# An attention kernel with values ahead of the next transposes, even filler, key-value latents first and four V buffers

## Chip, core and metric

One core of a Trainium2 chip. Its engines run side by side and meet at semaphores: TensorE (PE, matrix products and transposes into PSUM), VectorE (DVE), ScalarE (ACT), GpSimd (POOL, which doesn't reach PSUM), and SyncE (SP), which issues DMAs; ACT issues some too. The metric is the time of one execution on the device in microseconds.

## The reference

Two layers of a decoder trunk, for a prompt of 1024 tokens and 8 sample tokens that share all weights. What matters here is the attention branch of the prompt:

```python
def mla_qk(c_q, c_kv, k_r, pos, q_norm_g, w_uq, kv_norm_g):
    q = (rms_norm(c_q, q_norm_g) @ w_uq).reshape(B, T, N_HEADS, QK_HEAD)
    q_rope = rope(q[..., QK_NOPE:], pos)
    lat = rms_norm(c_kv, kv_norm_g)
    k_rope = rope(k_r[:, :, None, :], pos)[:, :, 0, :]
    ...
def mla_prompt(q_nope, q_rope, lat, k_rope, w_uk, w_uv):
    k_nope = jnp.einsum('bsc,chd->bshd', lat, w_uk)
    v = jnp.einsum('bsc,chd->bshd', lat, w_uv)
    def one_block(args):
        s = (q_nope . k_nope + q_rope . k_rope) * SM_SCALE
        s = jnp.where(k_pos[None, :] <= q_pos[:, None], s, -jnp.inf)
        p = jax.nn.softmax(s, axis=-1)
        return jnp.einsum('bhqk,bkhd->bqhd', p, v)
```

`c_q` (384 wide), `c_kv` (256) and `k_r` (32) are products of the layer's input with columns of `w_in`; the result is gated by a sigmoid-gated product (`ag`). The sample tokens attend to a paged cache; a pooling branch, the output products and layer norms follow.

## The kernel before

**Precision.** Every operand is held as a high and a low part (`XH`, `XL`; `CNH`, `CNL`; `KH`, `KL`; `QH`, `QL`; `PTH`, `PTL`), and a product is three products. ACT writes a high part, DVE subtracts for the low one.

**Weights** stream through a ring of four slots. SP loads a piece (`slab`), POOL splits it into high and low (`split`, L437), PE uses it in `unit` (L514) or `fill` (L533) and frees the slot (`w_used`). The order of `SLABS` is the order on all three engines.

**Latents and gates** (L685 to L704). Six units of 72 products make three query latents, two key-value latents and the rotary key; four more make the gates. Units alternate between two sets of three PSUM banks; a unit waits until the set is free (`unit_free`). ACT copies each latent to `CR` and its square to `SQ`; DVE adds squares; `squares` on PE sums over partitions; ACT takes roots; DVE takes the reciprocal and scales (L1165 to L1171), ACT and DVE make the parts; for each gate ACT takes a sigmoid, DVE multiplies and frees the banks.

**Values stage** (L706 to L726, L911 to L936). For each of 8 token blocks PE transposes latents and makes V; ACT copies the high part to `VSTG` (two buffers), copies `OUTT`, and issues three DMAs, one of them the spill of `VSTG` to HBM.

**The attention loop**, once for each of 4 head pairs in each of 2 layers (a pass). A pass has 16 blocks n: two heads of 8 blocks of 128 queries; block j of a head has (j+1)x128 keys. What each engine does, in the order written out by hand:

- PE (L741 to L757): `scores` 0 and 1, 24 filler products, then for each n `turn(n)` (transposes of the normalised block), `scores(n+2)`, at even n from 2 `values(n/2-1)`, and filler by `FILL_AT`. The filler is a product of the later mixing stage (144 products a pass), in six chunks that share one PSUM bank; ACT evacuates a chunk to `FST` and issues its DMA (`fill_evac`). After the loop: `keys_unit` of the next pair, `values(7)`, two query units.
- ACT (L972 to L993), iteration n: copies block n-2's transposes (`PTH`), takes the exponential of block n (`PB`), at even n from 4 copies `OB`, and at some n evacuates filler.
- DVE (L1230 to L1254), iteration n: reciprocal `RC` of n-1; mask, row maximum `MX` and `NB` of block n; `PTL` of block n-2 in one or two parts; at even n from 4 `ON`.
- POOL (L470 to L490): the normalising multiply of each block by `RC`, weight splits between.

`turn(n)` waits for POOL's multiply n and for `PTL` of n-1, whose PSUM banks it overwrites; `PTH` at even n waits for `values(n/2-1)`, which reads the buffer.

## Time and profile before

| | |
|---|---|
| median of 3 runs | 2287.74 us (2281.82 to 2289.15) |
| the profiled execution, whole | 2287.42 us |
| its span | 2285.5 us |
| mean granted clock of PE | 0.966 |
| busy: PE / DVE / ACT / POOL | 2051.3 / 910.4 / 508.6 / 755.3 us |
| chain that ended last: PE / DVE / issue / ACT | 78% / 11% / 5% / 2% |

The span runs from the first to the last instruction; the rest of the execution lies around it. Busy shares are averages over stages of different kinds, so the prediction reads single stages. In a timeline a bracket behind a row is the engine's idle time ahead of it and what ended that.

### The profile page before, as it was taken

Reading aid. Unit: us, or ns where it says so; the run is one execution under the profiler, and the core shown is the slowest. Engines: PE = TensorE matmul, PEld = TensorE weight load, DVE = VectorE, ACT = ScalarE, POOL = GpSimd, SP = SyncE. Lnnn points to the kernel's source line nnn. Section 1 sums busy time; section 2 is a strip of 40 time slices with the busy share of each in tenths; the row PEclk is TensorE's granted clock in tenths of the full one; section 3 lists DMA queues with packets and bytes.
Section 4 is the critical chain, followed back from the end, with each engine's and each line's share of the span. In section 5 each row is a group of like instructions: output and inputs, shape, how many; then the busy total and the mean of one; then the engine's idle time right before and its main releaser. Section 6 shows DMA issues by size and latency. Waiting matters only on the chain.

```text
span 2285.5 us, 33778 instructions
## 1 busy us (share of the span) xinstructions
PE 2051.3 (90%) x12406; PEld 1856.9 (81%) x12406; DVE 910.4 (40%) x1488; ACT 508.6 (22%) x895; POOL 755.3 (33%) x761
## 2 busy tenths in 40 slices
PE   2998898889998999999869988898799999999995
PEld 2997788774398999999869878788626989999994
DVE  7064555552155111421251645555423541133216
ACT  3122444441010100200121234444311110120002
POOL 5332333230034333443253233234200433334434
PEclk9999999998999999999979999999899999999997
DMA  3214011117312221111111231012461122211121
GB/s 113 61 42 148 26 55 60 54 55 235 135 44 64 79 74 55 42 46 51 47 31 45 68 117 57 26 55 66 155 213 54 49 86 65 74 42 47 50 62 76
DMA packets 90956, 167.08 MB, mean 73 GB/s; under 512 B 11641, under 2 KB 36489, under 8 KB 90415
## 3 DMA queue, kind: packets, MB, share of 16 engines
q1 hardware_dynamic: 74244, 135.43, 19.3%
q10 hardware_dynamic: 16572, 29.89, 3.5%
q8 instruction: 76, 1.25, 0.2%
q14 instruction: 64, 0.52, 0.1%
HBM read 141.74 MB, written 24.00 MB: 73 GB/s over the span
## 4 chain that ended last, share of the span: by engine, by line
PE 78%; DVE 11%; issue 5%; ACT 2%; DMA 2%; SPq 1%; ACTq 1%; DVEq 0%; POOL 0%; POOLq 0%
PE PS L525 53%; PE PS L546 6%; PE PS L568 4%; PE PS L616 3%; PE PS L646 2%; PE PS L579 2%; PE PS L603 2%; DVE MX L1239 2%; DVE PTL L1246 2%; PE PS L619 1%; PE PS L671 1%; DVE RT L1167 1%; DMA LATN<-out_lat_s 1%; PE PS L585 1%; DVE PS L1238 1%
## 5 line engine op out<-in xcount | busy, mean ns | idle before, releaser
L444 POOL CAST WH<-RAW 128x512 fp32r<-128x512 f32 (+3 forms) x296 | 192.4, 650 | 1079.4 <-DMA RAW<-in_wstream 1079.4
L446 POOL TENSOR_TENSOR WL<-RAW,WH 128x512 fp32r<-128x512 f32 (+3 forms) x296 | 381.9, 1290 | 23.9
L525 PE MATMUL PS<-XH,WH 128*128 128x344 f32 x1632 | 352.3, 324 | 13.9 <-DVEq L1349 5.5
L525 PE MATMUL PS<-XH,WL 128*128 128x344 f32 x1632 | 349.0, 322 | 0.0
L525 PE MATMUL PS<-XL,WH 128*128 128x344 f32 x1632 | 348.9, 322 | 0.0
L525 PEld LDWEIGHTS PS<-XH,WH 128*128 128x128 f32 x1632 | 275.9, 190 | 18.1 <-DVEq L1349 7.2
L525 PEld LDWEIGHTS PS<-XH,WL 128*128 128x128 f32 x1632 | 276.9, 190 | 0.0
L525 PEld LDWEIGHTS PS<-XL,WH 128*128 128x128 f32 x1632 | 276.3, 190 | 0.0
L467 POOL TENSOR_SCALAR PB<-PB,RC 128x128 f32<-128x128 f32 (+7 forms) x128 | 95.6, 747 | 346.6 <-DVE RC L1233 346.6
L579 PE MATMUL PS<-IDENT,PB 128*128 128x128 f32 x416 | 70.5, 284 | 77.6 <-DVE PTL L1246 77.6
L579 PEld LDWEIGHTS PS<-IDENT,PB 128*128 128x128 f32 x416 | 47.5, 143 | 96.8 <-issue 94.9
L546 PE MATMUL PS<-XH,WH 128*128 128x344 f32 x384 | 126.0, 328 | 0.0
L546 PE MATMUL PS<-XH,WL 128*128 128x344 f32 x384 | 122.7, 320 | 0.0
L546 PE MATMUL PS<-XL,WH 128*128 128x344 f32 x384 | 122.6, 319 | 0.0
L988 ACT ACTIVATE PB<-PS,NB 128x128 f32<-128x128 f32 (+7 forms) x128 | 94.9, 742 | 120.8 <-DVE NB L1240 119.8
L855 ACT ACTIVATE PTH<-PS 128x512 fp32r<-128x512 f32 (+1 forms) x192 | 87.3, 489 | 144.2 <-PE PS L603 116.7
L1373 DVE TENSOR_TENSOR SGP<-PS,SGP 128x1032 f32<-128x1032 f32 x16 | 19.7, 1233 | 246.4 <-PE PS L525 246.4
L1239 DVE TENSOR_REDUCE MX<-PS 128x1 f32<-128x128 f32 (+7 forms) x128 | 97.0, 757 | 4.4
L454 POOL TENSOR_TENSOR HT<-HT,GB 128x1024 f32<-128x1024 f32 (+1 forms) x27 | 70.1, 2611 | 75.1 <-ACT HT L868 63.1
L1246 DVE TENSOR_TENSOR PTL<-PS,PTH 128x512 fp32r<-128x512 f32 (+3 forms) x128 | 74.7, 584 | 48.5 <-ACT PTH L855 48.5
L603 PE MATMUL PS<-PTH,VSP 128*128 128x256 f32 x320 | 83.5, 292 | 3.1 <-DVE PTL L1250 3.1
L568 PE MATMUL PS<-KH,QH 128*128 128x512 f32 (+1 forms) x192 | 75.2, 392 | 8.4 <-DVEq L1212 8.2
(212 smaller groups left out, 3561.2 us busy)
## 6 DMA issues: line engine op xcount, KB each, us to landing
RAW<-in_wstream SPq DMA_DIRECT2D x232, 256.0 KB, 2.7
PGR<-in_pages SPq DMA_DIRECT2D x96, 320.0 KB, 4.9
PGA<-in_pages SPq DMA_DIRECT2D x32, 320.0 KB, 4.6
spill_g<-FST ACTq DMA_DIRECT2D x48, 172.0 KB, 1.9
SGL<-spill_g ACTq DMA_DIRECT2D x16, 516.0 KB, 4.4
spill_v<-VSTG ACTq DMA_DIRECT2D x16, 512.0 KB, 2.8
VSP<-spill_v SPq DMA_DIRECT2D x8, 1024.0 KB, 5.8
out_y_all<-HT SPq DMA_DIRECT2D x8, 512.0 KB
```

The source lines that it names most:

```text
L444: pool.tensor_copy(WH[:, slot, 0:size], RAW[:, slot, 0:size]).then_inc(w_high[slot], 1)
L446: pool.tensor_tensor(WL[:, slot, 0:size], RAW[:, slot, 0:size], f(WH[:, slot, 0:size]), ALU.subtract).then_inc(w_split[slot], 1)
L467: pool.tensor_scalar(PB[:, n % 2, 0:keys], PB[:, n % 2, 0:keys], RC[:, n:n + 1], 1.0, ALU.mult, ALU.mult).then_inc(nm_done, 1)
L525: last = nc.tensor.matmul(PS[:, 3 * par + c, 0:CH], w[:, slot, at], x(k)[:, c * CH:(c + 1) * CH], start=(k == 0 and n == 0), stop=(k == kt ...
L546: last = nc.tensor.matmul(PS[:, FILL_BANK, 0:CH], w[:, slot, (k % 4) * P:(k % 4 + 1) * P], x[:, k, c * CH:(c + 1) * CH], start=(step == 0) ...
L568: last = nc.tensor.matmul(score_banks(n)[:, c:c + w], q[:, h, j * P:(j + 1) * P], k[:, h, c:c + w], start=(m == 0), stop=(m == 2))
L579: last = nc.tensor.transpose(PS[:, 6, kb * P:(kb + 1) * P], PB[:, n % 2, kb * P:(kb + 1) * P], IDENT[:])
L603: last = nc.tensor.matmul(PS[:, o_bank(g), lo:2 * P], VSP[:, kb, h * P:(h + 1) * P], pt[:, kb, lo:2 * P], start=(kb == 0 and m == 0), stop ...
L855: return nc.scalar.activation(dst, src, ACT.Copy)
L988: nc.scalar.activation(PB[:, n % 2, 0:keys], score_banks(n)[:, 0:keys], ACT.Exp, bias=NB[:, n:n + 1], scale=SCALE, accum_out=SUM[:, n:n + ...
L1239: own(v.tensor_reduce(MX[:, n:n + 1], row[:, 0:(j + 1) * P], AX_X, ALU.max))
L1246: v.tensor_tensor(PTL[:, 0:w, c0:c0 + P], PS[:, 6, 0:w * P].rearrange("p (k c) -> p k c", c=P), f(PTH[:, 0:w, c0:c0 + P]), ALU.subtract).t ...
```

## The change

**Latents.** The two key-value latents are the first two units, the rotary key the third, the query latents the last three. `squares`, roots, sums, scalings and parts follow in the new order: three key-value squares after units 3 and 4, three query squares after gates 0 and 1. DVE scales the key-value latents ahead of gate 0 and the query latents between gates 1 and 2. The values stage waits for the key-value parts alone; the query units wait for the rest.

**V.** `VSTG` and its semaphores become four.

**Loop.** On PE `values(n/2-1)` stands ahead of `turn(n)`. The filler is 8 products for each n from 0 to 14, and its evacuations stand at n = 1, 4, 7, 10, 13, 16. On DVE `PTL` of block n-2 is first in iteration n. On POOL the next keys' weights are split at n = 9, both query slabs after the loop. SP gets some extra semaphore increments.

```diff
@@ -53,7 +53,7 @@
-SLABS = ([("c", 0, KD, 4, 1)] + [("c", n, KD, 2, 1) for n in range(1, 6)]
+SLABS = ([("c", KQ, KD, 4, 1)] + [("c", n, KD, 2, 1) for n in (*range(KQ + 1, KQ + KC + 1), *range(KQ))]
@@ -71,6 +71,8 @@
+ROPE_UNIT = KC
+LATENTS = ((0, KQ), (1, KQ + 1), (3, 0), (4, 1), (5, 2))
@@ -168,7 +170,7 @@
-        VSTG = at("VSTG", 19 * ROW, [P, 2, PAIRS, 4, V_DIM], F32R)
+        VSTG = at("VSTG", 19 * ROW, [P, 4, PAIRS, 4, V_DIM], F32R)
@@ -236,7 +238,8 @@
-        vs_out, fill_out, gate_in = ([sem(n + "0"), sem(n + "1")] for n in ("vs_out", "fill_out", "gate_in"))
+        vs_out = [sem(f"vs_out{k}") for k in range(4)]
+        fill_out, gate_in = ([sem(n + "0"), sem(n + "1")] for n in ("fill_out", "gate_in"))
@@ -290,9 +293,8 @@
-        FILL_AT = {-1: (0, 24), 0: (24, 36), 1: (36, 48), 2: (48, 60), 3: (60, 72), 4: (72, 78), 5: (78, 84),
-                   6: (84, 90), 7: (90, 96), 8: (96, 108), 9: (108, 120), 10: (120, 132), 11: (132, 144)}
-        FILL_EVAC = {1: 0, 3: 1, 5: 2, 9: 3, 11: 4, 13: 5}
+        FILL_AT = {-1: (0, 24)} | {n: (24 + 8 * n, 32 + 8 * n) for n in range(15)}
+        FILL_EVAC = {1: 0, 4: 1, 7: 2, 10: 3, 13: 4, 16: 5}
@@ -358,10 +362,12 @@
-                    for b in range(2):
-                        sp.wait_ge(vs_out[b], 64 * l + 64 + 1)
+                    for b in range(4):
+                        sp.wait_ge(vs_out[b], 32 * l + 32 + 1)
+                    sp.sem_inc(spare, 1)
...
+                    sp.sem_inc(spare, 1)
@@ -479,15 +485,11 @@
-                        if n == 5:
+                        if n == 9:
...
-                        if n == 13:
-                            split(l, after + 1, only=0)
-                        if n == 15:
-                            if i < PAIRS - 1:
-                                split(l, after + 2)
-                            else:
-                                split(l, after + 1, only=1)
+                    split(l, after + 1)
+                    if i < PAIRS - 1:
+                        split(l, after + 2)
@@ -675,29 +677,33 @@
 
                 def squares(n):
 
-                    par, c = divmod(n, 3)
-                    pe.wait_ge(sq_sum, 2 * l + par + 1)
+                    part, c = divmod(n, 3)
+                    pe.wait_ge(sq_sum, 2 * l + part + 1)
                     if n >= 2:
                         pe.wait_ge(rt_ready, 6 * l + n - 1)
-                    nc.tensor.matmul(PS[:, 6 + n % 2, 0:CH], ONES[:], SQ[:, (KQ - 1, KQ + KC - 1)[par], c * CH:(c + 1) * CH],
+                    nc.tensor.matmul(PS[:, 6 + n % 2, 0:CH], ONES[:], SQ[:, (KQ + KC - 1, KQ - 1)[part], c * CH:(c + 1) * CH],
                                      start=True, stop=True).then_inc(ss_done, 1)
 
                 for s in range(B_G):
                     unit(l, s, rows(XH), rows(XL))
-                    if s >= 4:
-                        squares(2 * (s - 4))
-                        squares(2 * (s - 4) + 1)
+                    if s == 3:
+                        squares(0)
+                        squares(1)
+                    if s == 4:
+                        squares(2)
 
                 for m in range(PAIRS):
                     unit(l, B_G + m, rows(XH), rows(XL))
                     if m == 0:
+                        squares(3)
                         squares(4)
+                    if m == 1:
                         squares(5)
 
                 pe.wait_ge(kr_ready, l + 1)
-                pe.wait_ge(cn_ready, (KQ + KC) * (l + 1))
-                pe.wait_ge(ch_ready, (KQ + KC) * (l + 1))
-                pe.wait_ge(cl_ready, (KQ + KC) * (l + 1))
+                pe.wait_ge(cn_ready, (KQ + KC) * l + KC)
+                pe.wait_ge(ch_ready, (KQ + KC) * l + KC)
+                pe.wait_ge(cl_ready, (KQ + KC) * l + KC)
                 pe.wait_ge(unit_free[0], q_of(l, B_G + 2) + 2)
                 slots = [piece_of(l, B_V, k) for k in range(KC)]
                 for slot, q in slots:
@@ -735,6 +741,8 @@
                     unit(l, B_F + 5 * i + 2, rows(CNH), rows(CNL))
 
                 keys_unit(0)
+                pe.wait_ge(ch_ready, (KQ + KC) * (l + 1))
+                pe.wait_ge(cl_ready, (KQ + KC) * (l + 1))
                 query_units(0)
                 for i in range(PAIRS):
                     r = l * PAIRS + i
@@ -742,11 +750,11 @@
                     scores(l, i, 1)
                     fill(l, i, -1)
                     for n in range(16):
+                        if n >= 2 and n % 2 == 0:
+                            values(r, n // 2 - 1)
                         turn(r, n)
                         if n + 2 < 16:
                             scores(l, i, n + 2)
-                        if n >= 2 and n % 2 == 0:
-                            values(r, n // 2 - 1)
                         fill(l, i, n)
                     pe.wait_ge(fill_free, 6 * r + 6)
                     if i < PAIRS - 1:
@@ -878,43 +887,63 @@
-                for s in range(KQ + KC):
+                def latent(s, k):
...
-                    copy(thirds(CR[:, s, :]), bank_set(s % 2))
-                    nc.scalar.activation(thirds(SQ[:, s, :]), bank_set(s % 2), ACT.Square).then_inc(unit_free[s % 2], 1)
+                    copy(thirds(CR[:, k, :]), bank_set(s % 2))
+                    nc.scalar.activation(thirds(SQ[:, k, :]), bank_set(s % 2), ACT.Square).then_inc(unit_free[s % 2], 1)
...
+                def root(n):
...
+                    part, c = divmod(n, 3)
+                    act.wait_ge(ss_done, 6 * l + n + 1)
+                    nc.scalar.activation(RT[:, 1 - part, c * CH:(c + 1) * CH], PS[:, 6 + n % 2, 0:CH], ACT.Sqrt, bias=EPSC[:],
+                                         scale=1.0 / (KV_LORA, Q_LORA)[part]).then_inc(rt_ready, 1)
...
+                def high(n):
...
+                    k = LATENTS[n][1]
+                    act.wait_ge(cn_ready, (KQ + KC) * l + n + 1)
+                    copy(CNH[:, k, :], CR[:, k, :]).then_inc(ch_ready, 1)
...
-                for n in range(6):
-                    par, c = divmod(n, 3)
-                    act.wait_ge(ss_done, 6 * l + n + 1)
-                    nc.scalar.activation(RT[:, par, c * CH:(c + 1) * CH], PS[:, 6 + n % 2, 0:CH], ACT.Sqrt, bias=EPSC[:],
-                                         scale=1.0 / (Q_LORA, KV_LORA)[par]).then_inc(rt_ready, 1)
...
-                for k in range(KQ + KC):
-                    act.wait_ge(cn_ready, (KQ + KC) * l + k + 1)
-                    copy(CNH[:, k, :], CR[:, k, :]).then_inc(ch_ready, 1)
-                    if k in (KQ - 1, KQ + KC - 1):
-                        gate(k // KQ)
+                latent(*LATENTS[0])
+                latent(*LATENTS[1])
+                latent(*LATENTS[2])
+                root(0)
+                root(1)
+                latent(*LATENTS[3])
+                root(2)
+                latent(*LATENTS[4])
+                high(0)
+                high(1)
+                gate(0)
+                root(3)
+                root(4)
+                root(5)
+                gate(1)
+                for n in range(KC, KQ + KC):
+                    high(n)
...
-                    act.dma_start(SPILL_V[t * P:(t + 1) * P, :], f(VSTG[:, t % 2]).rearrange("p i s d -> p (i s d)")
-                                  ).then_inc(vs_out[t % 2], 16)
+                    act.dma_start(SPILL_V[t * P:(t + 1) * P, :], f(VSTG[:, t % 4]).rearrange("p i s d -> p (i s d)")
+                                  ).then_inc(vs_out[t % 4], 16)
...
-                        act.wait_ge(vs_out[par], 64 * l + 16 * (t // 2) + 1)
-                        copy(values_high(VSTG[:, par]), PS[:, t % 3, :].rearrange("p (i x d) -> p i x d", i=PAIRS, x=2)
+                        act.wait_ge(vs_out[t % 4], 32 * l + 16 * (t // 4) + 1)
+                        copy(values_high(VSTG[:, t % 4]), PS[:, t % 3, :].rearrange("p (i x d) -> p i x d", i=PAIRS, x=2)
@@ -1130,21 +1159,20 @@
-                for par, k in ((0, 1), (0, 2), (1, 4)):
...
-                    dve.wait_ge(unit_free[k % 2], q_of(l, k) + 2)
-                    dve.wait_ge(unit_free[1 - k % 2], q_of(l, k - 1) + 2)
-                    last = v.tensor_tensor(SQ[:, k, :], SQ[:, k, :], SQ[:, k - 1, :], ALU.add)
-                    if k == 1:
-                        own(last)
-                    else:
-                        last.then_inc(sq_sum, 1)
+                def sum_squares(n):
...
+                    (s, k), (before, other) = LATENTS[n], LATENTS[n - 1]
+                    dve.wait_ge(unit_free[s % 2], q_of(l, s) + 2)
+                    dve.wait_ge(unit_free[before % 2], q_of(l, before) + 2)
+                    return v.tensor_tensor(SQ[:, k, :], SQ[:, k, :], SQ[:, other, :], ALU.add)
...
+                sum_squares(1).then_inc(sq_sum, 1)
...
-                products(dve, l, 5)
-                v.tensor_tensor(thirds(T1[64:96, :]), bank_set(1, 96, P), thirds(TAB[96:P, :]), ALU.mult)
-                own(v.tensor_tensor(thirds(T2[64:96, :]), bank_set(1, 64, 96), thirds(TAB[64:96, :]), ALU.mult))
-                dve.sem_inc(unit_free[1], 1)
+                products(dve, l, ROPE_UNIT)
+                v.tensor_tensor(thirds(T1[64:96, :]), bank_set(0, 96, P), thirds(TAB[96:P, :]), ALU.mult)
+                own(v.tensor_tensor(thirds(T2[64:96, :]), bank_set(0, 64, 96), thirds(TAB[64:96, :]), ALU.mult))
+                dve.sem_inc(unit_free[0], 1)
@@ -1162,28 +1190,42 @@
-                for par, lo, hi in ((0, 0, KQ), (1, KQ, KQ + KC)):
-                    dve.wait_ge(rt_ready, 6 * l + 3 * par + 3)
-                    own(v.reciprocal(RT[:, par, :], RT[:, par, :]))
-                    for k in range(lo, hi):
-                        v.scalar_tensor_tensor(out=CR[:, k, :], in0=CR[:, k, :], scalar=GL[:, k:k + 1], in1=RT[:, par, :],
+                def scaled(part):
...
+                    lo, hi = ((0, KC), (KC, KQ + KC))[part]
+                    dve.wait_ge(rt_ready, 6 * l + 3 * part + 3)
+                    own(v.reciprocal(RT[:, 1 - part, :], RT[:, 1 - part, :]))
+                    for _, k in LATENTS[lo:hi]:
+                        v.scalar_tensor_tensor(out=CR[:, k, :], in0=CR[:, k, :], scalar=GL[:, k:k + 1], in1=RT[:, 1 - part, :],
...
-                    gate(par)
...
+                def low(n):
...
+                    k = LATENTS[n][1]
+                    dve.wait_ge(ch_ready, (KQ + KC) * l + n + 1)
+                    v.tensor_tensor(CNL[:, k, :], CR[:, k, :], f(CNH[:, k, :]), ALU.subtract).then_inc(cl_ready, 1)
...
+                own(sum_squares(3))
+                scaled(0)
+                sum_squares(4).then_inc(sq_sum, 1)
+                low(0)
+                low(1)
+                gate(0)
+                gate(1)
+                scaled(1)
+                gate(2)
+                for n in range(KC, KQ + KC):
+                    low(n)
+                gate(3)
...
-                for k in range(KQ + KC):
-                    dve.wait_ge(ch_ready, (KQ + KC) * l + k + 1)
-                    v.tensor_tensor(CNL[:, k, :], CR[:, k, :], f(CNH[:, k, :]), ALU.subtract).then_inc(cl_ready, 1)
-                gate(2)
-                gate(3)
-                dve.wait_ge(cn_ready, (KQ + KC) * (l + 1))
...
-                        last = v.tensor_tensor(VSTG[:, t % 2, :, 1 + x, :],
+                        last = v.tensor_tensor(VSTG[:, t % 4, :, 1 + x, :],
...
-                                               f(VSTG[:, t % 2, :, 3 * x, :]), ALU.subtract)
+                                               f(VSTG[:, t % 4, :, 3 * x, :]), ALU.subtract)
@@ -1228,16 +1270,6 @@
 
                     own = Chain(dve, own_v["mx"], 32, r)
                     for n in range(18):
-                        if 1 <= n <= 16:
-                            dve.wait_ge(ex_done, 16 * r + n)
-                            v.reciprocal(RC[:, n - 1:n], SUM[:, n - 1:n]).then_inc(rc_done, 1)
-                        if n < 16:
-                            h, j = BLOCKS[n]
-                            row = score_banks(n)
-                            dve.wait_ge(sc_done, 16 * r + n + 1)
-                            own(v.tensor_tensor(row[:, j * P:(j + 1) * P], row[:, j * P:(j + 1) * P], MASK[:], ALU.add))
-                            own(v.tensor_reduce(MX[:, n:n + 1], row[:, 0:(j + 1) * P], AX_X, ALU.max))
-                            v.tensor_scalar(NB[:, n:n + 1], MX[:, n:n + 1], -SCALE, None, ALU.mult).then_inc(mx_done, 1)
                         m = n - 2
                         if m >= 0:
                             j = BLOCKS[m][1]
@@ -1250,6 +1282,16 @@
+                        if 1 <= n <= 16:
+                            dve.wait_ge(ex_done, 16 * r + n)
+                            v.reciprocal(RC[:, n - 1:n], SUM[:, n - 1:n]).then_inc(rc_done, 1)
+                        if n < 16:
+                            h, j = BLOCKS[n]
+                            row = score_banks(n)
+                            dve.wait_ge(sc_done, 16 * r + n + 1)
+                            own(v.tensor_tensor(row[:, j * P:(j + 1) * P], row[:, j * P:(j + 1) * P], MASK[:], ALU.add))
+                            own(v.tensor_reduce(MX[:, n:n + 1], row[:, 0:(j + 1) * P], AX_X, ALU.max))
+                            v.tensor_scalar(NB[:, n:n + 1], MX[:, n:n + 1], -SCALE, None, ALU.mult).then_inc(mx_done, 1)
```

## Rows read from the trace of the kernel before

**Rows 1.** PE's waits over the run: line, releaser, us in total, times, longest.
```profile
PE PS L579 <- DVE PTL L1246: 77.6, 72, 2.5
...
PE PS L525 <- DVE OT L1161: 5.0, 3, 2.1
```

**Rows 2.** Busy time by engine from `turn` 0 to `turn` 15, pair 2.
```profile
382.12:439.73 57.61, 47.91 (x317) 43.65 (x314) 32.00 (x84) 26.78 (x63) 20.29 (x27) 1.00 0.09 28
```

**Rows 3.** PE timeline, end of pair 2: start us, us, operation, idle before.
```profile
435.91 0.63 PE L579 MATMUL PS<-IDENT,PB 128*128 128x128 f32 x4 [2.53 <-DVE PTL L1246]
...
439.73 0.63 PE L579 MATMUL PS<-IDENT,PB 128*128 128x128 f32 x4 [1.50 <-DVE PTL L1246]
...
443.47 0.28 PE L603 MATMUL PS<-PTH,VSP 128*128 128x256 f32 x1
...
445.29 0.68 PE L525 MATMUL PS<-CNH,WH 128*128 128x344 f32 x3
```

**Rows 4.** DVE timeline, end of pair 2.
```profile
433.76 1.22 DVE L1239 TENSOR_REDUCE MX<-PS 128x1 f32<-128x1024 f32 x1
435.01 0.15 DVE L1240 TENSOR_SCALAR NB<-MX 128x1 f32<-128x1 f32 x1
435.08 0.68 DVE L1246 TENSOR_TENSOR PTL<-PS,PTH 128x512 fp32r<-128x512 f32 x1
435.68 0.41 DVE L1250 TENSOR_TENSOR PTL<-PS,PTH 128x256 fp32r<-128x256 f32 x1
436.44 0.16 DVE L1233 RECIPROCAL RC<-SUM 128x1 f32<-128x1 f32 x1 [0.34 <-ACT PB L988]
...
441.02 0.69 DVE L1246 TENSOR_TENSOR PTL<-PS,PTH 128x512 fp32r<-128x512 f32 x1 [0.51 <-ACT PTH L855]
```

**Rows 5.** ACT timeline, start and end of pair 2.
```profile
382.41 0.46 ACT L855 ACTIVATE FST<-PS 128x344 f32<-128x344 f32 x1 [1.11 <-PE PS L546]
382.90 0.34 ACTq L958 DMA_DIRECT2D spill_g<-FST  x1
383.29 0.28 ACT L855 ACTIVATE PTH<-PS 128x128 fp32r<-128x128 f32 x1 [0.42 <-ACT FST L855]
...
430.44 1.01 ACT L988 ACTIVATE PB<-PS,NB 128x896 f32<-128x896 f32 x1
...
431.56 0.38 ACT L855 ACTIVATE OB<-PS 64x256 f32<-64x256 f32 x1
431.96 0.87 ACT L855 ACTIVATE PTH<-PS 128x512 fp32r<-128x512 f32 x2
435.20 1.11 ACT L988 ACTIVATE PB<-PS,NB 128x1024 f32<-128x1024 f32 x1 [2.37 <-DVE NB L1240]
...
440.39 1.09 ACT L855 ACTIVATE PTH<-PS 128x512 fp32r<-128x512 f32 x2 [0.75 <-PE PS L579]
```

**Rows 6.** DVE's maximum of 128 keys in pair 2, form by form: busy us, mean ns.
```profile
L1239 DVE TENSOR_REDUCE MX<-PS 128x1 f32<-128x128 f32 x1 | 0.3, 291 | 0.0
```

**Rows 7.** POOL timeline: the normalising multiply of block 15, pair 2.
```profile
436.80 1.13 POOL L467 TENSOR_SCALAR PB<-PB,RC 128x1024 f32<-128x1024 f32 x1 [3.00 <-DVE RC L1233]
```

**Rows 8.** The page's costliest groups: a weight piece's low part, mean ns.
```profile
L446 POOL TENSOR_TENSOR WL<-RAW,WH 128x512 fp32r<-128x512 f32 (+3 forms) x296 | 381.9, 1290 | 23.9
```

**Rows 9.** Chain that ended last, in order of time: a unit of 72 products.
```profile
118.58 11.39 PE PS L525 x72
```

**Rows 10.** PE timeline at the gates of layer 0.
```profile
157.13 0.74 PE L525 MATMUL PS<-XH,WH 128*128 128x344 f32 x3 [2.11 <-DVE OT L1161]
```

**Rows 11.** ACT timeline at the gates of layer 0.
```profile
153.48 1.28 ACT L889 ACT_TABLE_LOAD   x1
```

**Rows 12.** A window of layer 1 behind an idle time (PEclk: granted clock).
```profile
1278.30:1281.70 3.40, 3.40 (x14) 3.40 (x13) 3.40 (x1) 0.00 (x0) 1.89 (x2) 0.50 0.00 0
```

**Rows 13.** ACT timeline in the values stage of layer 0.
```profile
192.19 0.60 ACT L855 ACTIVATE VSTG<-PS 128x512 fp32r<-128x512 f32 x1 [2.75 <-DMA spill_v<-VSTG]
...
194.78 0.60 ACT L855 ACTIVATE VSTG<-PS 128x512 fp32r<-128x512 f32 x1 [1.68 <-issue]
```

13 lines of the change are left out of this document (8 added, 5 removed).

## Prediction

> **What bounds the kernel now.** I read the head of the page first (span 2285.5 us, TensorE (PE) busy for most of it, so only its idle time can be won), then PE's own waits over the whole run. The longest group by far is `turn` (L579) waiting for the low-part subtraction PTL on VectorE (DVE, L1246), 77.6 us in 72 waits, so 9.7 us in each of the 8 passes over a head pair; the gates' units wait 5.0 us for OT [rows 1]. Third, one pass at undisturbed clock (pair 2 of layer 0): from `turn` 0 to `turn` 15 it takes 57.61 us, in which PE is busy 47.91, DVE 32.00, ScalarE (ACT) 26.78 [rows 2]. No engine is full; the loop is held by a chain of hand-overs. Fourth, the timelines of one step. `turn` 14 starts at 435.91, 0.83 after the first PTL of block 13 began at 435.08 [rows 3, 4]. That PTL did not wait for its data: it stood behind mask, row maximum and NB of block 15 (maximum 433.76, NB 435.01), which waited for PE's scores. So today a step is: turn, scores, mask and maximum, PTL, next turn. The exponential runs beside PTL and costs that chain nothing.
>
> **The change in the attention loop.** DVE now takes PTL(m) ahead of RC(m+1) and of mask, maximum, NB of block m+2. PE no longer waits for a maximum before PTL. But the order on ACT is unchanged: the copy PTH(n-1) stands behind the exponential of block n, and that exponential needs NB(n), which now stands behind PTL(n-2). This closes a serial loop that before was open: PTL(n-2), RC, mask, maximum, NB on DVE; exponential n, whatever ACT does at the end of its iteration, PTH(n-1); PTL(n-1). I cost it from rows, from the end of one PTL to the end of the next:
> - hand-overs: RC 0.10 (0.16 long at 436.44, less its overlap with the next), mask 0.34 (my estimate: as a 128-wide maximum with its hand-over), maximum's tail 0.03, NB to exponential 0.19 (435.01 to 435.20): together 0.66 [rows 4, 5];
> - M, the maximum: 0.29 at 128 keys, 1.22 at 1024, on a line between [rows 4, 6];
> - E, the exponential: 1.01 at 896 keys and 1.11 at 1024, on the line through them down to 0.47 at 256, plus 0.12 where OB follows (430.44, OB at 431.56) [rows 5];
> - X, what follows it on ACT: OB 0.40 (431.56 to 431.96) at even n from 4; evacuating a filler chunk 0.88 (FST 382.41, its DMA issue 382.90, PTH 383.29) at n = 4, 7, 10, 13 by the new table [rows 5];
> - H, PTH to PTL: 0.63 at four or more blocks (440.39 to 441.02), down to 0.41 for two and 0.31 for one (my estimates, less by the 0.11 a block of the exponential) [rows 4, 5];
> - L, PTL: 0.60 for four blocks (435.08 to 435.68); with the second part 0.82 to 1.20; 0.22 for one (estimates: a part's duration runs with its width like the maximum's, less the 0.08 by which two overlap) [rows 4].
>
> ```
> n    M     E     X     H     L    0.66+sum
> 2   0.56  0.57   -    0.41  0.34   2.54
> 3   0.69  0.68   -    0.52  0.47   3.02
> 4   0.82  0.91  1.28  0.63  0.60   4.90
> 5   0.96  0.89   -    0.63  0.82   3.96
> 6   1.09  1.12  0.40  0.63  0.94   4.84
> 7   1.22  1.11  0.88  0.63  1.08   5.58
> 10  0.56  0.69  1.28  0.41  0.34   3.94
> 11  0.69  0.68   -    0.52  0.47   3.02
> 12  0.82  0.91  0.40  0.63  0.60   4.02
> 13  0.96  0.89  0.88  0.63  0.82   4.84
> 14  1.09  1.12  0.40  0.63  0.94   4.84
> 15  1.22  1.11   -    0.63  1.08   4.70
> ```
> Two steps go by another path. RC(k), too, now stands behind PTL(k-1), so the normalising multiply on GpSimd (POOL) comes in series: RC to its start 0.36 and 1.13 at 1024 keys [rows 4, 7], 0.15 to PE (a PTL of 0.68 lets `turn` start at 0.83 [rows 3, 4]). For k=7: 1.63, then turn to PTH 0.66 (439.73 to 440.39) [rows 3, 5], H, L 1.20: 4.12. For k=8 `values(3)` comes first: 1.82 long (443.47 to 445.29 for the same 16 products [rows 3]), with 0.15 ahead and `turn`, PTH and PTL of one block, 0.9, behind: in all 2.85. The 14 steps sum to 57.2. Ahead of them, `turn` 0 to PTL(0): 1.17 to PTH(0) (382.12 to 383.29 [rows 2, 5]), then about 0.5: 1.7. Behind them RC(15) and the multiply, 1.6, before `turn` 15. Total 60.5 against 57.61: **+2.9 a pass, +23.1 for eight**. `values` ahead of `turn` at even n is covered: it runs while the multiply makes the block that `turn` waits for. At every step but the eighth PE's work (8 fillers 1.26, scores up to 1.5, turn up to 0.8, values up to 1.8) is shorter than the loop beside it, so evening the fillers buys nothing.
>
> What is late next: after the loop `turn` 15, the keys unit, `values(7)` and two query units follow on PE alone, as today; they start 2.9 later.
>
> **Splits and loads.** POOL splits the next keys at n = 9 and both query slabs after n = 15. A piece of four tiles costs POOL 1.29 for its low part and about half of that for the high one [rows 8], so the two query pieces of three tiles take some 3 us after the last multiply, while PE has 0.8 of turn, 2.9 of keys unit (a quarter of a unit of 11.39 [rows 9]) and 1.8 of values ahead of the first query unit. Cost nothing; if the cover were gone, up to 3 a pass. SP's loads keep their order; the slots of the last two free one and two steps later than now, still before `turn` 15. The extra semaphore increments on SP cost nothing seen.
>
> **Latents first.** PE's own work is the same: six units, four gates and six squares a layer. Now the gate units wait 5.0 us (the longest 2.11 at 157.13) since DVE has a long queue of reciprocals and scalings between the gates [rows 1, 10]. In the new order DVE has little to do when gate 0's unit ends: table load 1.28, sigmoid and multiply about 1.1 each, done 3.5 us after it, 8 ahead of the end of the next unit (11.39), when its banks are wanted; gate 1's waits for a square and a root more, 4.7, so 6.7 ahead [rows 9, 11]. The 5.0 go. In layer 1 the 2.1 idle was followed by a stretch at half clock, 3.4 us, of which half is lost: 1.7 [rows 12]. Sum -6.7. Two more table loads on ACT each layer lie within those 6.7 us (1.28 each). The values stage then starts as soon as PE is there, as now.
>
> **Four V buffers.** ACT takes 2.6 a block by its own work; only one block a layer waits for a spill: idle 2.75 where its neighbour has 1.68, 1.07 more, and I take as much for layer 1 [rows 13]. The rest of the stage is ACT's issues, which stay. **-2.1** for two. Bounds: 0 (OUTT's own buffers wait instead) and 2.1.
>
> **Sum**, against the profiled run's own 2287.4 (span 2285.5; the median is 2287.7): 2287.4 + 23.1 - 6.7 - 2.1 = **2301.7**. Bounds of the loop's term: 0.1 us of error on each of 14 steps is 11 us over eight passes, so +12 to +34.
>
> **Rivals.**
> - *ACT's filler issue is free.* If the DMA issue and its gap (0.39 of the 0.88) don't hold the next copy, four steps a pass get shorter: -12.5, so **2289.2**, within the noise. Against it: PTH in the row comes only after the issue [rows 5]. The Trainium skill, "DMA: Bandwidth & Descriptors", section Issuing engines are not separate DMA queues, calls the sequencer's time to start a DMA usually small beside the DMA; by that rule this rival holds, while the row here shows 0.34 on the path.
> - *Faster: PTL first sets PE free.* The mechanism is what the 77.6 us suggest: PTL no longer waits behind a maximum, and the exponential is out of the way by the time the copy's data come. Then a step is the longer of PE's work (2.2 to 3.9) and the path of k=7 above, RC, multiply, turn, H, L (2.2 to 4.1): 47.5 for the 14 steps, 50.8 in all, -6.8 a pass, so 2287.4 - 54.4 - 8.8 = **2224**. It decides once the serial loop is under 54.3 for the 14 steps, 0.2 less in each. For it: neither DVE nor ACT is busy much over half the pass [rows 2]. Against it: both run their queues in order, and the code puts the exponential ahead of the copy.
> - *The clock.* PE will idle about 2.9 us ahead of `turn` 15, 2.5 ahead of `turn` 7. Today an idle time of 2.1 ahead of a gate unit in layer 1 is followed by 3.4 us at half clock [rows 12], and half of the passes lose their clock so once. If four passes more than today get it, 4 x 1.7, and all eight a second one at `turn` 7, partly covered, 8 x 1.2: up to +16.4, **2318**.
> - *The gates don't gain.* The new order only moves the idle time: +8.8, **2310.5**.
>
> **How the numbers follow.** Forecast 2302, chance 0.54; free issue 0.14; clock 0.16; no gain at the gates 0.06; faster 0.10. Range 2285 to 2318: it takes in the free issue, most of the clock case and the loop's bounds, and leaves out the fast case and the tails. About 0.3% (7 us) is what a measurement of this kernel can tell from no change. Slower by more: 0.75 (forecast, clock, gates, less a little); same: 0.14; faster: 0.11.
>
> **What would show it.** In the trace after: exponential n starting only after PTL(n-2), and PTH(n-1) right behind it, so that DVE and ACT alternate; `turn` 15 about 60.5 after `turn` 0; PE's waits at `turn` put down to the POOL multiply and not to PTL, and above 100 us in all; no wait at the gates; no ACT wait for spill_v. I'm wrong if PTH starts while the exponential of the next block is still to come, or if a pass is shorter than 57.6.

## The result and the profile after

The changed kernel takes 2332.85 us (median of 4 runs, 2327.55 to 2335.32); the kernel before, run beside it, 2286.2. The ratio is 1.0203 (95% interval 1.0177 to 1.0228): slower by 2.0%, 31 us more than the 2302 forecast and above the range. The profiled execution took 2331.88 (span 2330.0), 44.5 more than that of before.

PE's waits of the changed kernel over the whole run (line, releaser, us in total, times, longest):

```profile
PE PS L581 <- POOL PB L473: 63.3, 62, 2.4
PE PS L770 <- DMA LATN<-out_lat_s: 25.0, 2, 12.7
```

These answer to [rows 1]. `turn` (now L581) no longer waits for PTL but for the multiply, as foreseen; the total is smaller than the 77.6 of before, and yet the kernel is slower. The gates' wait for OT is gone. The second line is new: L770 is the first product of the sample stage with UKT, and it waits about 12.5 us in each layer for a DMA.

Passes, windows from `turn` 0 to `turn` 15 of pairs 2 and 3 of layer 0 (columns as in [rows 2]: length, then busy time and count of PE, PEld, DVE, ACT, POOL, granted clock, DMA share, GB/s):

```profile
384.84:447.06 62.22, 51.96 (x317) 46.16 (x314) 31.75 (x86) 26.85 (x63) 17.48 (x24) 0.95 0.07 24
466.95:526.90 59.95, 49.72 (x317) 43.51 (x314) 31.65 (x86) 26.84 (x63) 19.76 (x24) 1.00 0.10 34
```

A pass at full clock takes 59.9 to 60.0; the eight are 59.9, 62.4, 62.2, 60.0 and 61.0, 62.3, 59.9, 61.0, mean 61.07. In the kernel before a pass at full clock takes 57.6, as in [rows 2], and the mean of the eight is 58.49, since five of the eight lose 1.3 to 1.6 us of clock ahead of the last `turn`. The hand-overs at the end of pair 2, DVE and then ACT (start us, us, operation, idle before):

```profile
435.31 0.69 DVE L1278 TENSOR_TENSOR PTL<-PS,PTH 128x512 fp32r<-128x512 f32 x1 [2.50 <-ACT PTH L864]
...
436.49 1.09 DVE L1293 TENSOR_REDUCE MX<-PS 128x1 f32<-128x896 f32 x1
437.62 0.15 DVE L1294 TENSOR_SCALAR NB<-MX 128x1 f32<-128x1 f32 x1
...
439.96 0.69 DVE L1278 TENSOR_TENSOR PTL<-PS,PTH 128x512 fp32r<-128x512 f32 x1 [0.20 <-ACT PTH L864]
...
441.29 1.22 DVE L1293 TENSOR_REDUCE MX<-PS 128x1 f32<-128x1024 f32 x1
```

```profile
437.81 1.01 ACT L1017 ACTIVATE PB<-PS,NB 128x896 f32<-128x896 f32 x1 [2.37 <-DVE NB L1294]
...
438.93 0.38 ACT L864 ACTIVATE OB<-PS 64x256 f32<-64x256 f32 x1
439.33 0.87 ACT L864 ACTIVATE PTH<-PS 128x512 fp32r<-128x512 f32 x2
```

Against [rows 4, 5] PTL now comes first on DVE, and everything else waits in a row: PTL at 435.31, maximum 436.49, NB 437.62, exponential 437.81, OB 438.93, PTH 439.33, the next PTL 439.96. DVE and ACT alternate; the serial loop of the prediction is there, piece by piece.

SyncE's DMA issues at the end of the last pass of layer 0, first before, then after (start us, us from the first to the last issue of the group; SPq: its DMA queue):

```profile
472.72 31.67 SPq L333 DMA_DIRECT2D RAW<-in_wstream  x3
509.78 4.15 SPq L381 DMA_DIRECT2D PGA<-in_pages  x8
514.13 0.58 SPq L389 DMA_DIRECT2D UKT<-in_ukt  x1
514.81 0.52 SPq L390 DMA_DIRECT2D UVF<-in_uvf  x1
515.62 0.29 SPq L393 DMA_DIRECT2D LATN<-out_lat_s  x1
```

```profile
482.95 42.09 SPq L337 DMA_DIRECT2D RAW<-in_wstream  x4
530.39 4.68 SPq L387 DMA_DIRECT2D PGA<-in_pages  x8
535.26 0.57 SPq L395 DMA_DIRECT2D UKT<-in_ukt  x1
535.93 0.51 SPq L396 DMA_DIRECT2D UVF<-in_uvf  x1
536.73 0.29 SPq L399 DMA_DIRECT2D LATN<-out_lat_s  x1
```

And the chain that ended last, in order of time, over the same place in the kernel after:

```profile
523.28 1.28 PE PS L548 x8
524.71 0.33 SPq L337
525.05 0.05 issue
525.16 0.48 SPq L382
...
536.73 8.92 DMA LATN<-out_lat_s
545.65 0.04 issue
545.69 2.51 PE PS L770 x11
```

PE's last eight fillers (L548, n = 14) free a weight slot at 524.56; only then does SP issue the last piece of slab B_H + 1 (L337). Behind it in SP's program stand the reads of the page ids (L382), eight page loads, UKT, UVF and LATN, and LATN lands at 545.65. In the kernel before, the last filler was at n = 11, and LATN was issued at 515.62, 21.1 us earlier. From `turn` 15 (526.90) to the UKT products it is now 18.8 us, where it was 6.9; in layer 1, 19.6 and 6.8.

**Where the 44.5 us are** (profiled executions): from the first `turn` 0 to the last `turn` 15 of a layer +11.1 and +14.2; from there to the UKT products +11.9 and +12.8; everything ahead of the first `turn` 0 -3.0, from layer 0's UKT products to layer 1's first `turn` 0 -1.5; the rest -1.0.

### The profile page after: what moved, and what is told of

It is laid out like the page before. It is cut to its first block, busy times and chain, and to the rows that moved or that the text cites. A ratio compares the mean times of both kernels' runs of the same rounds, so it can differ in the third digit from the quotient of the medians.

```text
span 2330.0 us, 33806 instructions
## 1 busy us (share of the span) xinstructions
PE 2071.6 (89%) x12406; PEld 1866.3 (80%) x12406; DVE 908.5 (39%) x1488; ACT 513.9 (22%) x899; POOL 757.4 (33%) x761
## 4 chain that ended last, share of the span: by engine, by line
PE 68%; DVE 11%; issue 8%; ACT 7%; ACTq 2%; DMA 1%; SPq 1%; POOL 1%; DVEq 0%; POOLq 0%
PE PS L527 54%; DVE MX L1293 4%; PE PS L618 3%; PE PS L648 2%; ACT PTH L864 2%; ACT PB L1017 2%; PE PS L548 2%; PE PS L605 1%; PE PS L621 1%; DVE PS L1292 1%; PE PS L673 1%; DVE PTL L1282 1%; DMA LATN<-out_lat_s 1%; ACT FST L864 1%; POOL PB L473 1%
## 5 line engine op out<-in xcount | busy, mean ns | idle before, releaser
L527 PEld LDWEIGHTS PS<-XH,WH 128*128 128x128 f32 x1632 | 276.1, 190 | 12.8 <-DVEq L1391 7.2
L548 PE MATMUL PS<-XH,WH 128*128 128x344 f32 x384 | 127.8, 333 | 13.4 <-ACT FST L864 13.4
L581 PE MATMUL PS<-IDENT,PB 128*128 128x128 f32 x416 | 74.2, 293 | 63.3 <-POOL PB L473 63.3
L548 PE MATMUL PS<-XH,WL 128*128 128x344 f32 x384 | 125.0, 325 | 0.0
L548 PE MATMUL PS<-XL,WH 128*128 128x344 f32 x384 | 124.5, 324 | 0.0
L581 PEld LDWEIGHTS PS<-IDENT,PB 128*128 128x128 f32 x416 | 46.1, 144 | 80.3 <-POOL PB L473 80.1
L460 POOL TENSOR_TENSOR HT<-HT,GB 128x1024 f32<-128x1024 f32 (+1 forms) x27 | 70.2, 2615 | 75.1 <-ACT HT L877 63.3
L548 PEld LDWEIGHTS PS<-XH,WH 128*128 128x128 f32 x384 | 73.7, 192 | 23.5 <-ACT FST L864 22.2
```

The lines of the kernel that those rows point to most:

```text
L460: pool.tensor_tensor(HT[0:n, t, :], HT[0:n, t, :], GB[0:n, :], ALU.mult).then_inc(ht_mul, 1)
L527: last = nc.tensor.matmul(PS[:, 3 * par + c, 0:CH], w[:, slot, at], x(k)[:, c * CH:(c + 1) * CH], start=(k == 0 and n == 0), stop=(k == kt ...
L548: last = nc.tensor.matmul(PS[:, FILL_BANK, 0:CH], w[:, slot, (k % 4) * P:(k % 4 + 1) * P], x[:, k, c * CH:(c + 1) * CH], start=(step == 0) ...
L581: last = nc.tensor.transpose(PS[:, 6, kb * P:(kb + 1) * P], PB[:, n % 2, kb * P:(kb + 1) * P], IDENT[:])
```

## Experiments

"Pass" below is `turn` 0 to `turn` 15 in the trace of the run, "between" is from there to the next `turn` 0. Medians in us; ratios to the kernel before, run beside each.

### 1. SP's sample loads first

```diff
-                slab(l, B_H)
-                slab(l, B_H + 1)
 ...
                 sp.dma_start(LATN[...], ...)
+                slab(l, B_H)
+                slab(l, B_H + 1)
```

> The changed kernel with one move on SP: the first sample's pages, UKT, UVF and LATN are issued ahead of the first two pooling slabs instead of behind them. Theory Q (these loads stand in SP's queue behind a slab that waits for the last filler products, which now end at n = 14 instead of 11): PE's wait for LATN falls from 25.0 us to under 2, the whole falls by 22 to 26 us, to about 2309. Rival (the loads are late because the DMA engines are busy or because the page identifiers are slow to read): the wait stays within 3 us of 25. The passes stay at 61.1 in both.

Measured 2304.52, ratio 1.0076 (1.0059 to 1.0093), 28.3 less than the changed kernel, a little more than the 22 to 26 expected. LATN is issued at 473.90, PE no longer waits for it at all, and the UKT products start 6.3 us after `turn` 15 in both layers. The queue on SP is the cause of that part.

### 2. The old filler table under the new orders

```diff
-        FILL_AT = {-1: (0, 24)} | {n: (24 + 8 * n, 32 + 8 * n) for n in range(15)}
+        FILL_AT = {-1: (0, 24), 0: (24, 36), ... 11: (132, 144)}
```

> The changed kernel with the filler, its evacuations and POOL's splits as before; values first, PTL first, latents first and four buffers stay. Theory Q: the last filler product is at n = 11 again, the LATN wait of 25 us goes. Theory S (the pass is held by PTL, maximum, exponential, copy in series): the filler is not what lengthens the pass; evacuations stand at five n inside the chain instead of four, so a pass is 61 to 63. Whole: 2308 to 2320. Rival E (the even filler is what costs the loop): passes fall back to 58.5, whole about 2288.

Measured 2309.92 (1.0089 to 1.0123). SP's order is that of the changed kernel, yet the UKT products start 6.9 after `turn` 15: the late filler is what held SP. Passes are 60.3 to 61.3, so under the new orders the even filler buys nothing in the loop, as forecast. It does shorten PE's wait ahead of `turn` 15 from 3.6 to 4.0 us to 2.4 us.

### 3. PTL first alone

The kernel before, with only PTL(n-2) moved ahead of RC, mask, maximum and NB on DVE.

> The kernel before with one change: on DVE PTL(n-2) ahead of RC(n-1) and of mask, maximum and NB of n. Theory S: this alone closes the serial loop, and values behind scores now holds up the copy at even n too: a pass goes from 58.5 to about 64 (steps of 5.4 at n = 4, 12, 14 and 5.7 at n = 6), whole about 2286 + 47 = 2333. Rival (PTL first frees PE, and the loss comes from PE's new order): PE's wait at turn falls below 77.6 us and the whole is at or under 2286.

Measured 2363.79 (1.0319 to 1.0353): +77, where +47 was expected. Passes are 66.0 to 67.6. ACT's timeline in it:

```profile
517.38 0.19 ACT L988 ACTIVATION_READ_ACCUMULATOR PB<-PS,NB 128x1 f32 x1
518.31 0.98 ACT L855 ACTIVATE PTH<-PS 128x512 fp32r<-128x512 f32 x2 [0.74 <-PE PS L603]
```

The exponential ends at 517.57, and the copy then waits 0.74 for PE's `values` (L603): at even m PTH overwrites what `values` of the group before reads, and PE's old order puts `values` behind `turn` and scores. My expectation left that out. So values ahead is what the new DVE order needs: with this filler the two together give a mean pass of 60.8 (experiment 2), PTL first without values ahead 66.8.

### 4. Latents and V buffers alone

The changed kernel with orders, filler and splits of before.

> The changed kernel with the attention loop, filler and splits as before: only latents first and four V buffers are left of the change. By the traces: no wait at the gates (5.0 us before), passes 58.5 as before, no LATN wait; 2286 less 5 to 7, about 2280. Rival: the gain is taken back later in the layer (clock, values stage): within 2 us of before.

Measured 2280.48, ratio 0.9975 (0.9963 to 0.9986), -6.2. Experiments 4 and 1 cut the way from the kernel before to the changed one into three steps, in medians: 2286.7 - 6.2 (latents, V) + 24.0 (loop: 2304.5 - 2280.5) + 28.3 (SP) = 2332.8. The steps are differences of neighbouring runs, so they add up whatever the cause; the causes are shown by the traces. In this run's trace the stretches ahead of the first `turn` 0 of each layer (from the start, and from layer 0's UKT products) are 4.4 us shorter each, and its passes 0.34 longer in the mean (58.83), since only one keeps its clock where three did.

### 5. DVE's old order under values ahead

> The changed kernel with one thing put back: on VectorE, mask, maximum and NB of block n stand ahead of PTL(n-2) again, as in the kernel before. Values ahead of the next transposes, the even filler, the latents' order and the four V buffers stay. Theory S (the serial loop over DVE and ACT, closed by PTL first, is what lengthened the pass): passes from turn 0 to turn 15 fall from 61.1 to about 58, PE's largest wait at the turn is put down to PTL again, exponential n starts before PTL(n-2) ends; LATN still lands late (some 12 us ahead of each layer's sample stage), so the whole is about 2332.9 - 8 x 3.1 = 2308 (2300 to 2316). Theory P (PE's new order, values ahead of the turn, lengthened it): passes stay at 60 to 61, 2325 to 2333.

Measured 2327.65 (1.0149 to 1.0185); passes 60.3 and 60.4. Theory P, and a miss for the claim that DVE's order alone is to blame. DVE and then PE in it:

```profile
403.93 1.23 DVE L1281 TENSOR_REDUCE MX<-PS 128x1 f32<-128x1024 f32 x1
405.19 0.15 DVE L1282 TENSOR_SCALAR NB<-MX 128x1 f32<-128x1 f32 x1
405.26 0.68 DVE L1288 TENSOR_TENSOR PTL<-PS,PTH 128x512 fp32r<-128x512 f32 x1
405.85 0.41 DVE L1292 TENSOR_TENSOR PTL<-PS,PTH 128x256 fp32r<-128x256 f32 x1
```

```profile
406.32 0.39 PE L605 MATMUL PS<-PTH,VSP 128*128 128x256 f32 x1 [1.51 <-DVE PTL L1292]
...
407.78 0.41 PE L581 MATMUL PS<-IDENT,PB 128*128 128x128 f32 x2
```

`values` waits 1.51 us for PTL, which stands behind the next maximum, and `turn` starts 1.46 later, after `values`. At every even n the time of `values` now lies between PTL and `turn`; before it lay beside DVE's maximum. The steps agree: against experiment 6 those that end at an even n are longer, from 0.5 us (n = 2) to 2.4 (n = 8), and the steps from `turn` 6, 8 and 14 are shorter, by 1.3 to 1.6.

### 6. Even filler alone, SP mended

Latents first, four V buffers, even filler, SP's sample loads first; PE's and DVE's orders as before.

> Latents first, four V buffers and the even filler with its splits, but PE's and DVE's orders in the loop as in the kernel before, and SP's page, UKT, UVF and LATN loads ahead of the last two filler slabs. What is measured is the even filler alone, against the kernel before with latents first and four V buffers (2280.5). Theory: at turn 15 the kernel before waits 1.5 us on PTL(13) with no filler to cover it in steps 12 to 15; evened out, eight filler products a step take part of it: passes 57.1 instead of 58.8, 2280.5 - 8 x 1.7 = 2267 (2260 to 2275). Rival: with eight filler products in every step some steps become bound by PE or by the evacuation of a chunk, and nothing is won: 2278 to 2286. If the sample stage's operands are late still, +24.

Measured 2255.23, ratio 0.9849 (0.9827 to 0.987), faster than the kernel before by 33. In a window of pair 2 (columns as above):

```profile
371.85:427.97 56.12, 48.76 (x317) 43.29 (x314) 32.01 (x84) 26.69 (x63) 18.91 (x25) 1.00 0.07 23
```

All passes are 56.0 to 56.1, against a mean of 58.8 in experiment 4, whose one pass at full clock takes 57.6: 1.6 of the gain is waits that are filled (1.7 was expected), the other 1.2 the clock, which no pass loses any more. The eight passes make 22.4 of the 25.3 us against experiment 4; another 2.6 lie between `turn` 15 and the UKT products, where LATN comes early. So the even filler is good under PE's and DVE's old orders. Values ahead costs 4.3 a pass on top of it (60.3, experiment 5); PTL first on top of both takes 0.4 off a pass at full clock (59.9), but its longer waits cost clock, and the mean is 61.1.

### 7. Copy ahead of the exponential

To break the serial loop at ACT: PTH(n-1), then the exponential of block n.

```diff
-                        m = n - 2
-                        if m >= 0:
+                        for m in ((), (), (0, 1))[n] if n < 3 else (n - 1,) if n < 17 else ():
                             ... copy PTH of block m
                         if n < 16:
                             ... exponential of block n
```

> The changed kernel with ACT's loop turned round: copy PTH(n-1) stands ahead of the exponential of block n, where now the exponential comes first. No arithmetic changes. Theory S says the serial loop (PTL(n-2), mask, maximum, NB, exponential n, PTH(n-1), PTL(n-1)) is broken by it. What is left is PTH(n-1), exponential n, RC, multiply, turn, PTH(n): with the rows' durations 2.5 to 4.4 us a step, 50.6 for 14 steps, a pass of about 54 instead of 61; 2332.9 - 8 x 7 = 2276 (2265 to 2295), the late LATN unchanged. The rival, that the pass is held by the multiply and the turn and not by the queue order of ACT, says 60 to 62 a pass, 2325 to 2340. A third: the later exponential only puts the wait on RC, which stands ahead of the mask on DVE, and the pass comes out at 57 to 58, 2305.

> Both mends together: copy PTH(n-1) ahead of the exponential on ACT, and SP's page, UKT, UVF and LATN loads ahead of the last two filler slabs. They act at different places (inside the passes; between the last turn and the sample stage), so the times should add: 2304.5 (SP's order alone) - 8 x 7 = 2248, range 2240 to 2268. If the first does nothing, 2305.

Measured 2368.09 (1.0312 to 1.0363) and, with SP mended, 2341.2 (1.0213 to 1.0244); passes 62.0 to 63.6. Both far off. ACT and DVE in the first:

```profile
415.66 0.88 ACT L864 ACTIVATE PTH<-PS 128x512 fp32r<-128x512 f32 x2 [2.35 <-PE PS L581]
416.42 1.01 ACT L1016 ACTIVATE PB<-PS,NB 128x896 f32<-128x896 f32 x1
...
417.55 0.38 ACT L864 ACTIVATE OB<-PS 64x256 f32<-64x256 f32 x1
```

```profile
417.96 0.42 DVE L1267 TENSOR_TENSOR ON<-PS,OB 64x256 f32<-64x256 f32 x1 [2.90 <-ACT OB L864]
418.31 0.67 DVE L1277 TENSOR_TENSOR PTL<-PS,PTH 128x512 fp32r<-128x512 f32 x1
```

PTH is done at 416.54, but PTL starts at 418.31. DVE stood for 2.90 us at ON, which is ahead of PTL in its queue and waits for OB; OB stood behind the exponential. PE also waited 42.6 us for filler chunks, evacuated a turn later than before. The loop was not broken, only led over another operation.

### 8. OB and evacuation moved ahead too

```diff
+                        if n >= 4 and n % 2 == 0:
+                            own_low(r, n // 2 - 2)
+                        if n in FILL_EVAC:
+                            fill_evac(l, i, FILL_EVAC[n])
                         for m in ...   # copy PTH, then the exponential
```

> As the run with copy PTH(n-1) ahead of the exponential and SP's sample loads first (2341.2), but the copy OB and the evacuation of a filler chunk, which ACT did after the exponential, now stand ahead of PTH(n-1). Why that run missed, by my reading of its trace: ON on VectorE stands ahead of PTL(n-1) in its queue and waits for OB, which waited for the exponential, so the serial loop stayed closed at every even n; and PE waited 42.6 us for filler chunks evacuated a turn later than before. If so, both go here: step = PTH, exponential, RC, multiply, turn, 2.5 to 4.4 us, a pass of 54 to 56 instead of 62 to 63, whole 2304.5 - 8 x 6 = 2256 (2244 to 2270). Rival: the multiply and the turn in series hold every step whatever ACT does, pass 60 or more, 2300 to 2340.

Measured 2255.91 (0.9844 to 0.9877), as expected; undisturbed passes 54.2 against 59.9. Moving three operations in one engine's queue, with no work added or taken, changed the kernel by 49 us (2304.5 to 2255.9). That shows the serial loop as the cause of the long pass under the new orders. The run moves OB and the evacuation together, so it doesn't tell how much of experiment 7's loss each of them held.

### 9. Two V buffers, and experiment 6 again

> The kernel with the even filler, the old orders on PE and VectorE, latents first and SP's sample loads first (2255.2 in another call, run again beside this one), with two V buffers in place of four. Theory A, as forecast: the wait for a spill, 1.07 us a layer, comes back: +2.1 us. Theory B, from the trace after (where the wait for a spill is gone, but one DMA issue a layer took 1.5 to 1.9 us in place of 0.46): the stall only moves between wait and issue, so the difference is 0 +- 1. Both are near what three rounds tell; the trace decides: the values stage from its first to its last product in each layer.

> The even filler with the old orders on PE and VectorE, latents first, four V buffers and SP's sample loads first, again, beside the two above and in more rounds: 2255 +- 3, a ratio of 0.985 to 0.987 to the kernel before. If it comes out above 2265, the first measurement was a chip's luck.

Measured 2253.57 (2251.44 to 2257.36) with two and 2254.13 (2251.9 to 2256.82) with four: no difference, but four runs of each, spread over 5 to 6 us, can't tell 2.1 us from nothing. The changed kernel's ACT in the values stage, to answer to [rows 13], and then that of the run with two buffers:

```profile
184.28 1.88 ACTq L937 DMA_DIRECT2D spill_v<-VSTG  x1
186.32 0.60 ACT L864 ACTIVATE VSTG<-PS 128x512 fp32r<-128x512 f32 x1 [3.08 <-PE PS L726]
188.25 0.46 ACTq L937 DMA_DIRECT2D spill_v<-VSTG  x1
```

```profile
185.13 1.56 ACTq L938 DMA_DIRECT2D spill_v<-VSTG  x1
186.88 0.60 ACT L865 ACTIVATE VSTG<-PS 128x512 fp32r<-128x512 f32 x1 [2.78 <-PE PS L727]
```

The wait for a spill is gone, but an issue of the same DMA held ACT for 1.88 us where its neighbours take 0.46. The slow issue is not the price of four buffers, since it comes with two as well. The traces say more than the medians. From PE's first transpose of the stage to its last, the six stages of the three traces with two buffers (the kernel before, experiment 3 and this one) take 20.2 to 20.7 us. With four buffers the sixteen stages that have a slow issue take 20.1 to 21.8, and the six that have none 19.2 to 19.3 (layer 0 of the run with four buffers here among them). So 1.1 us a layer, the forecast 1.07, is won where no issue is slow, as far as six stages show; in most stages the slow issue takes it.

### 10. Filler where PE waits

Experiment 8 with 12 filler products after `turn` 6, 16 after `turn` 14, 4 in steps 0, 1 and 4. Four chunks, not two as the expectation has it, are evacuated a step later.

> The run with copy, OB and evacuation ahead of the exponential (2255.9), with filler products moved to where PE idles most: 12 in place of 8 after turn 6, 16 after turn 14, 4 in steps 0, 1 and 4, which have no idle time; the evacuation of two chunks a step later. PE's work is the same. In that run the undisturbed pass is 54.2, but in 5 of 8 passes idle time of 1.8 ahead of turn 7 is followed by about 1.3 us more in step 7, and idle time of 2.2 ahead of turn 15 by a keys unit of 4.6 in place of 3.1 us. Theory C (the half clock follows those idle times): they shrink to 1.2 and 0.9, the granted clock stays up, all passes 54 to 54.5, keys units 3.1: 8 us in the passes and 9 between them, 2239 (2232 to 2248). Rival: the half-clock stretches come at other idle times instead, or the extra products only lengthen steps 6 and 14: 2252 to 2262.

Measured 2243.52, ratio 0.9793 (0.9774 to 0.9813), the fastest of all. Windows of pair 2 and of the keys unit behind it, in experiment 8 and here (columns as above; the clock is the third number from the end):

```profile
373.28:429.17 55.89, 49.26 (x317) 44.98 (x314) 33.05 (x86) 26.54 (x65) 17.50 (x24) 0.97 0.08 25
429.17:433.20 4.03, 4.03 (x20) 4.03 (x21) 1.29 (x2) 1.08 (x2) 2.86 (x4) 0.64 0.16 60
```

```profile
369.11:423.38 54.27, 47.96 (x316) 43.45 (x314) 33.03 (x86) 26.39 (x65) 17.43 (x24) 1.00 0.07 24
423.38:427.40 4.02, 4.02 (x29) 4.02 (x30) 1.29 (x2) 1.13 (x3) 2.60 (x4) 1.00 0.41 107
```

With the waits of 1.8 and 2.2 us filled, the clock stays up: the pass is 1.6 shorter, the same 4 us do 29 products in place of 20, and "between", 21.4 to 21.5 in five cases of six, is 19.9 in all. The waits ahead of `turn` 7 and 15 are 1.21 and 0.92 (1.20 ahead of `turn` 15 in the first pass of each layer). The gain was 12 us of the 17 expected. My expectation had counted 5 of 8 passes of experiment 8 as losing clock at `turn` 7; its trace has that in two (steps of 5.94 and 5.92 us for 4.59). In the profiled executions the passes gain 5.4 us in all and the stretches between them 7.8.

The last pass of each layer keeps a long step, 4.40 and 4.41 us at n = 9 for 2.64 in the other passes. POOL and then PE in layer 0:

```profile
474.93 0.61 POOL L452 CAST WH<-RAW 128x512 fp32r<-128x512 f32 x1
...
477.55 1.27 POOL L454 TENSOR_TENSOR WL<-RAW,WH 128x512 fp32r<-128x512 f32 x1
478.80 0.58 POOL L475 TENSOR_SCALAR PB<-PB,RC 128x384 f32<-128x384 f32 x1
```

```profile
479.43 0.55 PE L583 MATMUL PS<-IDENT,PB 128*128 128x128 f32 x3 [1.59 <-POOL PB L475]
```

This is the split at n = 9. In the last pass the slab behind it is the first of the pooling branch, two pieces of four tiles, and it holds POOL for 3.9 us; for a keys slab, with pieces of one tile, it is 1.6. The multiply of block 10 stands behind it and `turn` 10 waits. Steps 9 and 10 together are 1.7 us longer than in the other passes, once a layer, now that the serial loop is open. In the changed kernel the loop hides nearly all of it: step 9 is 4.23 for 3.82 us, step 10 2.76 for 3.06.

## Why the prediction was wrong

**The step that failed** is in *Splits and loads*: "SP's loads keep their order; the slots of the last two free one and two steps later than now, still before `turn` 15. ... cost nothing". Both slots free three steps later, not one and two: the products that end them move from n = 10 and 11 to n = 13 and 14. They still free before `turn` 15 (the last at 524.56, `turn` 15 at 526.90). The conclusion, that this costs nothing, is what failed: I asked whether the weights would be in time, and not what else stands behind those two loads on SP. In the last pair that is the whole operand set of the sample stage, some 20 us of reads, issues and landing. The filler's end moved from n = 11 to 14, and the row moved with it. Price: 28.3 us in experiment 1, 24.6 in the profiled executions. The trace of before held the sign of it, among PE's waits (columns as in [rows 1]):

```profile
PE PS L762 <- DMA LATN<-out_lat_s: 1.4, 2, 0.8
```

PE already waited for LATN there, so there was no slack. The Trainium skill, "DMA: Bandwidth & Descriptors", section Issuing engines are not separate DMA queues, calls the sequencer's time to start a DMA usually small beside the DMA. For a single DMA the trace agrees: an issue of a page load takes 0.33 to 0.70 us, and the load lands 4.7 us after it. But a row of them in one queue adds up: eight id reads and eight issues held SP from 525.16 to 535.1 before UKT could be issued.

**The loop's term was right, its size in part by luck.** Forecast +23.1, measured 24.0 in medians. The prediction counts a step from the end of one PTL to the end of the next. Counted so in the first pass, all fourteen steps, k=7 (4.06 for 4.12) and k=8 (2.92 for 2.85) among them, are within 0.1 us of the table, and their sum is 56.7 for 57.2; 1.8 us lie ahead of them (1.7 forecast) and 1.45 behind (1.6). The mechanism and its costs are right. The whole pass at full clock, 59.9, is 0.6 below the 60.5 forecast, so by itself the loop makes 18.7 of the 23.1. That the total comes so near is luck: in the profiled executions lost clock adds 1.9 in the passes (the mean pass grew by 2.58, 20.6 in eight) and 4.7 in the stretches between them, 25.3 in all. A window of step 7 of pair 1 in the changed kernel:

```profile
329.40:336.20 6.80, 5.82 (x25) 5.83 (x26) 2.92 (x9) 2.60 (x7) 1.29 (x2) 0.51 0.01 4
```

Clock 0.51 for 6.8 us, behind a wait for the multiply; the step takes 7.1 in place of 4.6. In layer 0 each of the first three pairs loses its clock once, at `turn` 7 (pairs 1 and 2) or in the keys unit behind `turn` 15 (pair 0: 21.5 between in place of 19.9). The clock rival named the right waits (2.15 us ahead of `turn` 7 and 2.36 ahead of `turn` 15, for 2.5 and 2.9 forecast), but clock lost beyond that of before comes to 6.6 us, not 16.4, and it is a part of the loop's 24.0, not on top of it.

**What I had wrong about the mechanism**, though it cost the number nothing: "values ahead is covered". It is, once PTL is first (experiment 2 against experiment 3). But against DVE's old order it costs 4.3 a pass (experiments 5 and 6), and "evening the fillers buys nothing" holds only inside the serial loop; outside it the even filler is worth 2.8 a pass.

**Latents first**: forecast -6.7. Experiment 4 gives -6.2 (3 to 8.5 by its interval) for latents and V together, with about as long a values stage as before, so the forecast stands within the interval. **Four V buffers**: forecast -2.1. The medians of experiment 9 can't tell it from 0. By the traces both bounds occur: a stage is 1.1 us shorter when no spill's issue is slow, and not shorter when one is, as in both layers of the changed kernel. That reason was not on the list. The price of the rival that the gates don't gain was wrong as well: 8.8 includes the V buffers' 2.1; the gates alone are 6.7.

**Its own tests.** Exponential only after PTL, PTH right behind it, waits at `turn` on the multiply, none at the gates, no ACT wait for spill_v: all seen. "Above 100 us in all" was wrong: the waits at `turn` come to 63.3, and FST adds 13.4 in 24 waits at the filler (L548). A pass at full clock has 10.2 us without PE (59.95 less 49.72), where before it had 9.7 [rows 2].

**Rivals.** Free filler issue: no; PTH comes 0.46 after the start of the issue (434.21 to 434.67), as in [rows 5]. "PTL first sets PE free" (2224) failed for the reason given against it, the queue order on ACT; with that order mended the pass is 54.2, not the 50.8 it claimed.

**Open.** The slow issue of a spill (1.4 to 2.3 us, in most values stages) moves between blocks from run to run; no run tells its cause. Why the same wait is followed by half clock in one pass and not in the next is open too. No run has PTL first under the even filler without values ahead, and none takes the split at n = 9 back alone.

## What to carry to other kernels

When a change moves the last use of a buffer later, list everything that stands behind its reload in the issuing queue, up to the next stage's operands, and not only the reload; such a queue should hold what is needed soonest first. In a loop over engines with in-order queues, write down the cycle of hand-overs with every operation that stands between them, small ones too: with only PTH moved, the loop stayed closed over OB, a copy of 0.4 us. Test each of several moves alone: here one part was worth 1.1% (2280.5 to 2255.2) once SP's order was mended, and the others hid it.
